# First group of the feed-forward part of a hybrid encoder step: combinations, row sums and row factors in another order

## The reference, cut to what matters

```python
def rmsnorm(x, g, eps=EPS):
    xf = x.astype(jnp.float32)
    y = xf * lax.rsqrt(jnp.mean(xf * xf, axis=-1, keepdims=True) + eps)
    return (y * g.astype(jnp.float32)).astype(x.dtype)

def layer_tail(x, attn, rw, attn_out_g, w_out, norm_ffn_g, w_gate, w_up, w_down):
    mix = jnp.concatenate([rmsnorm(attn, attn_out_g), rw], axis=-1)
    h = x + mix @ w_out
    u = rmsnorm(h, norm_ffn_g)
    return h + (jax.nn.silu(u @ w_gate) * (u @ w_up)) @ w_down
```

## Time and profile before

| | |
|---|---|
| median of 3 runs | 1844.28 us (1843.1 to 1844.76) |
| profiled execution, its own time | 1845.74 us |
| its span, first to last instruction | 1844.0 us |
| mean granted TensorE clock | 0.979 |
| PE busy | 1749.5 us, 95% of the span |
| DVE busy | 959.6 us, 52% |
| POOL busy | 601.8 us, 33% |
| ACT busy | 402.3 us, 22% |

### The profile page before, as it was taken

How to read it: one execution, slowest core, us unless ns; L and a number is a source line. 1 busy time by engine, 2 the same in 40 slices (tenths; PEclk the granted TensorE clock), 3 DMA queues, 4 the chain that set the end, 5 groups by cost and what they waited for, 6 DMA issues and landing times.

```text
span 1844.0 us, 34696 instructions
## 1 busy us (share of the span) xinstructions
PE 1749.5 (95%) x14741; PEld 1327.4 (72%) x14741; DVE 959.6 (52%) x1766; ACT 402.3 (22%) x933; POOL 601.8 (33%) x418
## 2 busy tenths in 40 slices
PE   5999999999997886999999999999999999999998
PEld 4566666666665554666666888888888888888887
DVE  2767767767766774665325344434333334535422
ACT  2333333334333233555001110111001000000000
POOL 3563664555455430001200122211222210734332
PEclk9999999999997888999999999999999999999999
DMA  9443344324322006110402011111011111333431
GB/s 367 142 148 106 88 132 139 97 91 152 99 70 73 8 7 174 47 47 1 186 23 94 23 46 46 46 46 34 35 46 46 46 46 64 123 95 115 141 99 55
DMA packets 80431, 159.00 MB, mean 86 GB/s; under 512 B 28731, under 2 KB 57227, under 8 KB 76054
## 3 DMA queue, kind: packets, MB, share of 16 engines
q1 hardware_dynamic: 76262, 115.81, 19.6%
q10 hardware_dynamic: 4016, 40.96, 6.3%
HBM read 128.60 MB, written 20.48 MB: 81 GB/s over the span
## 4 chain that ended last, share of the span: by engine, by line
PE 50%; DVE 1%; issue 0%; ACT 0%; DVEq 0%
PE psum L2333 45%; PE psum L2312 5%; PE psum L2322 0%; DVE u_sum L2559 0%; DVE mixT L2560 0%; DVE u_sum L2564 0%; PE psum L2328 0%; DVE mixT L2543 0%; DVE rb L2576 0%; DVE hid L2540 0%; DVE hid L2539 0%; DVE hid L2535 0%; DVE yout L2676 0%; DVE part L2675 0%; DVE part L2625 0%
## 5 line engine op out<-in xcount | busy, mean ns | idle before, releaser
L2333 PE MATMUL psum<-mixT,wA 128*128 128x264 f32 x1408 | 338.6, 389 | 1.9 <-DVE rb L2576 1.5
L2333 PEld LDWEIGHTS psum<-mixT,wA 128*128 128x128 f32 x1408 | 269.0, 191 | 48.8 <-DVE rb L2576 1.7
L2333 PE MATMUL psum<-u_sum,wA 128*128 128x264 f32 x1232 | 298.7, 388 | 0.5 <-DVE u_sum L2559 0.5
L461 PE MATMUL psum<-wsl,xt 128*128 128x368 f32 (+1 forms) x1092 | 283.1, 449 | 8.3 <-DMA wsl<-in_w_in 5.0
L2333 PEld LDWEIGHTS psum<-u_sum,wA 128*128 128x128 f32 x1232 | 235.4, 191 | 41.6 <-issue 0.9
L461 PEld LDWEIGHTS psum<-wsl,xt 128*128 128x128 f32 (+1 forms) x1092 | 149.6, 171 | 90.8 <-issue 17.4
L2490 POOL TENSOR_TENSOR wA<-wA 128x512 f32<-128x512 f32 x22 | 27.9, 1268 | 427.9 <-DMA wA<-in_w_gate 231.3
L2333 PE MATMUL psum<-hid,wA 128*128 128x264 f32 x528 | 120.2, 386 | 2.1 <-DVE hid L2627 1.5
L2333 PEld LDWEIGHTS psum<-hid,wA 128*128 128x128 f32 x528 | 100.2, 190 | 19.9 <-issue 2.8
L1956 PE MATMUL psum<-kT,qT 104*128 104x346 f32 (+7 forms) x224 | 77.6, 464 | 10.1 <-DMA kT<-scratch_kT 9.4
L1297 POOL TENSOR_TENSOR Ls<-Lraw,con 128x512 f32<-128x512 f32 x45 | 49.1, 1100 | 95.3 <-ACT Lraw L964 65.2
(11 more groups left out here) (351 smaller groups left out, 2840.7 us busy)
## 6 DMA issues: line engine op xcount, KB each, us to landing
wsl<-in_w_in ACTq DMA_DIRECT2D x27, 1472.0 KB, 6.7
wA<-in_w_down SPq DMA_DIRECT2D x32, 704.0 KB, 4.1
wA<-in_w_gate SPq DMA_DIRECT2D x22, 512.0 KB, 4.3
wA<-in_w_up SPq DMA_DIRECT2D x22, 512.0 KB
mixed<-proj SPq DMA_DIRECT2D x8, 784.0 KB
xt<-in_x_tiles SPq DMA_DIRECT2D x9, 512.0 KB, 6.0
wsl<-in_w_in SPq DMA_DIRECT2D x3, 1472.0 KB, 11.5
out_y<-hid SPq DMA_DIRECT2D x1, 4224.0 KB, 13.9
```

The costliest lines, as they stand in the source:

```text
L461: return pe.matmul(out, lhsT, rhs, start=start, stop=stop)
L2333: ins = pe.matmul(pb[bank][:, 0:NW], left(k), right(k), start=first and k == 0, stop=k == depth - 1, skip_group_check=not first)
```

## The change

Three edits in `tail`, all around the first two groups. (1) DVE does the first group's three combinations before the last block's squares; the squares and the means become `row_means`, called behind the third combination. (2) PE makes the row sums behind the first group's last product, no longer before its closes. (3) The factors are spread by PE transposes of `row_ms` itself, broadcast along a row, against the identity, into banks 5 to 7 and behind X of the second group, not before it; ACT's nine diagonals go. PE signals after four, eight and nine transposes, DVE copies each bank when it is told, and Y, Z and W of the second group wait for the first, second and third copy.

```diff
         def row_factors():
-            pe.wait_ge(s["diag_ok"], TT_)
+            pe.wait_ge(s["r_ok"], 1)
             for t, w in enumerate(width):
-                last = pe.matmul(pb[4 + t // 4][:, t % 4 * P:t % 4 * P + w], ones[0:w, :], diag[0:w, t, 0:w], start=True, stop=True)
-            last.then_inc(s["rb_ps"], 1)
+                last = pe.transpose(pb[5 + t // 4][:, t % 4 * P:t % 4 * P + w], row_ms[0:w, t:t + 1].broadcast_to([w, P]), ident[0:w, 0:w])
+                if t % 4 == 3 or t == TT_ - 1:
+                    last.then_inc(s["rb_ps"], 1)
...
                 if it == 1:
                     pe.wait_ge(s["h_ok"], 3 * KD)
-                    row_factors()
-                    pe.wait_ge(s["rb_ok"], 3)
                 if it >= 2:
                     pe.wait_ge(s["x_done"], it - 1)
                 product(X, left(A11), half(B11u), KH, "p1_ps")
+                if it == 1:
+                    row_factors()
...
+                if it == 1:
+                    pe.wait_ge(s["rb_ok"], 1)
                 if it >= 2:
                     pe.wait_ge(s["y_done"], it - 1)
                 product(Y, left(sw[b][:, 1]), half(T2u), KH, "p6_ps")
...
+                if it == 1:
+                    pe.wait_ge(s["rb_ok"], 2)
                 if it >= 2:
                     pe.wait_ge(s["z_done"], it - 1)
                 product(Z, left(S3), half(B12u), KH, "p7_ps")
                 if it == 0:
-                    row_sums()
                     pe.wait_ge(s["u_hi"], KH)
                 else:
                     pe.wait_ge(s["s1_ok"], u + 1)
+                    if it == 1:
+                        pe.wait_ge(s["rb_ok"], 3)
...
                 product(W, left(sw[b][:, 2]), half(B22u), KH, "w_ps", first=False)
+                if it == 0:
+                    row_sums()
...
                 act.activation(p1_[it % 2][:, :], pb[X][:, 0:NW], ACT.Copy).then_inc(s["p1_ok"], 1)
-                if it == 0:
-                    act.wait_ge(s["r_ok"], 1)
-                    for t in range(TT_):
-                        act.activation(diag[:, t, :], ident, ACT.Copy, scale=row_ms[:, t:t + 1]).then_inc(s["diag_ok"], 1)
...
         tt(T4u, B21u, T2u, ALU.subtract).then_inc(s["t4_ok"], 1)
-        squares(KD - 1)
-        full = TOK // P
-        dve.wait_ge(s["ssq_ps"], 1)
...
+
+        def row_means():
+            squares(KD - 1)
+            full = TOK // P
+            dve.wait_ge(s["ssq_ps"], 1)
...
         def row_factors():
-            dve.wait_ge(s["rb_ps"], 1)
             for n in range(0, TOK, 512):
                 w = min(512, TOK - n)
-                dve.tensor_copy(rb[:, n:n + w], pb[4 + n // 512][:, 0:w]).then_inc(s["rb_ok"], 1)
+                dve.wait_ge(s["rb_ps"], n // 512 + 1)
+                dve.tensor_copy(rb[:, n:n + w], pb[5 + n // 512][:, 0:w]).then_inc(s["rb_ok"], 1)
             dve.wait_ge(s["rb_ok"], 3)
...
                 named(tt(u3, W, u3, ALU.add), "c22_ok", it + 1)
                 if it == 0:
+                    row_means()
                     row_factors()
```

More of the change, by code:

```diff
@@ L2186, in tail @@
     g11 = sb("g11", [P, NW])
-    diag = hid_[:, 9 * TOK:9 * TOK + TT_ * P].rearrange("p (t n) -> p t n", t=TT_)
     ones = hid_[:, 6 * TOK:6 * TOK + P]
@@ L2212, in tail @@
     Alo, Ahi = (w[:, 0:FB * P].rearrange("p (k n) -> p k n", k=FB) for w in wA)
-    names = """x_in0 x_in1 x_in2 g_in in0 in1 in2 in3 lo_read u_hi1 waited zero ps_done h_ok sq_ok acc_ok ssq_ps ms_ok r_ok diag_ok rb_ps rb_ok u_lo u_hi h_st
+    names = """x_in0 x_in1 x_in2 g_in in0 in1 in2 in3 lo_read u_hi1 waited zero ps_done h_ok sq_ok acc_ok ssq_ps ms_ok r_ok rb_ps rb_ok u_lo u_hi h_st
         t1_ok t2_ok t3_ok t4_ok w_in0 w_in1 s1_ok s2_ok s3_ok s4_ok p1_ps p6_ps p7_ps p5_ps x_ps z_ps w_ps
@@ L2564, in _ @@
         tt(T4u, B21u, T2u, ALU.subtract).then_inc(s["t4_ok"], 1)
-        squares(KD - 1)
-        full = TOK // P
-        dve.wait_ge(s["ssq_ps"], 1)
-        dve.tensor_scalar(row_ms[:, 0:full], pb[6][:, 0:full], 1.0 / D, EPS, ALU.mult, ALU.add).then_inc(s["ms_ok"], 1)
-        dve.tensor_scalar(row_ms[0:width[-1], full:], pb[6][0:width[-1], full:TT_], 1.0 / D, EPS, ALU.mult, ALU.add
-                          ).then_inc(s["ms_ok"], 1)
+        def row_means():
+            squares(KD - 1)
+            full = TOK // P
+            dve.wait_ge(s["ssq_ps"], 1)
+            dve.tensor_scalar(row_ms[:, 0:full], pb[6][:, 0:full], 1.0 / D, EPS, ALU.mult, ALU.add).then_inc(s["ms_ok"], 1)
+            dve.tensor_scalar(row_ms[0:width[-1], full:], pb[6][0:width[-1], full:TT_], 1.0 / D, EPS, ALU.mult, ALU.add
+                              ).then_inc(s["ms_ok"], 1)
         def row_factors():
-            dve.wait_ge(s["rb_ps"], 1)
             for n in range(0, TOK, 512):
                 w = min(512, TOK - n)
-                dve.tensor_copy(rb[:, n:n + w], pb[4 + n // 512][:, 0:w]).then_inc(s["rb_ok"], 1)
+                dve.wait_ge(s["rb_ps"], n // 512 + 1)
+                dve.tensor_copy(rb[:, n:n + w], pb[5 + n // 512][:, 0:w]).then_inc(s["rb_ok"], 1)
             dve.wait_ge(s["rb_ok"], 3)
```

## The result

The changed kernel took 1834.33 us in the median of 4 runs (1833.48 to 1837.66), against 1844.52 for the kernel before (1843.1 to 1845.67): a ratio of 0.9948, 95% interval 0.9931 to 0.9966. The profiled execution took 1834.33 us itself, with a span of 1832.5 us and a mean granted clock of 0.981 (0.979 before). The forecast was 1832.8 in a range of 1830.9 to 1836.4.

A forecast was written before the change was run, and what follows sets the result against it. PE bounds the FFN part; the third group's start sets the end. Waits and cheaper factors (4.8 us) plus low clock (6.6) give 11.46 us: profiled execution 1834.3, median 1.46 lower, 1832.8 us; range 1830.9 to 1836.4.

The forecast's parts named there:

- The path: After the third group starts, PE waits for nothing changed; program end moves with that start, from 1038.59 to 1027.13.
- the stretch: PE's time from the start of p7, the first group's last undisturbed product, to the third group's start; 11.46 us less.
- The closes: First group: X, Z, W closes no longer wait for squares; 8.39 us become 5.34, wait of 3.79 becomes 0.39.
- The sums: Row sums behind the first group's last close: no wait, full clock, 1.91 us instead of 3.70.
- The chain to Y: Second group, between X and Y: means, power, transposes, first copy; 0.91 wait, 0.99 transposes, 0.50 wait, replacing 3.83 us.
- The clock: First two groups: 6.6 of the 11.46 us gained are low clock, granted 0.50 after PE's idle times; 1.00 after the change.
- Rival 1: Clock falls again between X and Y of the second group: 1834.6 us for one fall, 1836.4 for two; chance 0.28.
- Rival 2: Cover for ACT's copy of X (0.64 us) or the squares (0.6) too thin: up to 1 us, 1833.8; no own chance.
- Rival 3: PE stays at 1.2 GHz from the sums through the second group and beyond: slower than before, 1851.8 us; chance 0.02.
- Rival 4: First group's closes still held behind the squares; only cheaper factors gain, 1.4 us, 1842.9; chance 0.03.
- The rule weighed: Trainium skill: transposes do not count as busy for the clock; between X and Y they would equal idle time.

The follow-up runs named there:

- the second profile: The kernel before, unedited, profiled again: 32.54 us from p7 of the first group to the third group, 3.20 less than in its first profile.
- the kernel with more sums: The changed kernel with 64 more one-column matmul calls (128 records) ahead of the nine row sums: 1861.92 us.
- the filled kernel before: The kernel before with eight idle matmul calls after p7 and three before the wait for the copies, so PE works through both waits: 1841.28 us, ratio 0.9982.

## Why the prediction was right, and where it was off

**The path.** That only the start of the third group counts held: 805.4 us behind it in both. Forecast 1027.13, measured 1027.03. Part of this closeness is luck: the sum took p7 at 1002.85 from the profile before, and the first profile after had it at the same time, while the next one had it at 1005.12. The length of the stretch, 24.28 forecast and 24.18 measured twice, is not luck.

**The closes.** Close of Z forecast at 1006.80, measured 1006.86; of W 1008.58 and 1008.71. The squares were hidden as said. From the end of u3 on DVE to PE's start it took 0.15 us, not 0.10.

**The sums.** Forecast 1.91 from the attention phase, measured 1.93 (1010.49 to 1012.42).

**The chain to Y.** Power forecast to end at 1014.62, measured 1014.69. I took 0.34 us from there to the first transpose, and it was 0.06: this is the term mis-sized, between its bounds of 0.03 and 0.34. The wait was 0.55 us (1014.20 to 1014.75), not 0.91. The transposes' rate was right, so Y came at 1016.27 for 1016.45.

**The clock.** The 6.6 us of low clock were real in the execution that the prediction read: its sums, closes, X and Y were all at full pace in the changed kernel. Filling the waits gave 4.6 us back against that execution, and the fall left over accounts for most of the rest; against the second profile it gave 1.4. The sum was off in two places. It took the falls of one execution as a fixed part of the kernel before; the second profile had 3.20 us less, so the gain is 8.4 to 11.6 by execution. And the forecast of the time was too low by 1.5 us for another reason: for the profiled execution it was 1834.3, and 1834.33 was measured, but for the median it took off 1.46 more, the distance of one execution before from its median. Nothing tied that distance to the kernel after, whose profiled execution was its own median. One reading was loose: the first fall came at 1007.88, 3.0 us into the wait of 3.56 and not behind it.

**Rival 1** did not occur in any of the seven profiled executions that have all three edits and no added sums, three of them with other work added. Whether it lies behind the longer runs that were not profiled (1837.66, 1839.48) stays open. **Rival 2's** covers held with 0.7 and 0.8 us. **Rival 3** had no trace of itself in the changed kernel. The kernel with more sums shows the half of it that the clock can be low with PE busy, 27.30 us at 1.2 GHz and 1861.92 us in all; the other half, that it does not come back behind products, was seen nowhere. **Rival 4** is excluded by the timeline.

**The rule weighed** (transpose-mode work does not count as busy for the clock, in the Trainium skill, "TensorE: Matmul & The Clock Gate", Part 4) does not hold for these 32-bit transposes: 72 of them in 7.85 us kept the granted clock at 1.00, and in the kernel with more sums it came back while transposes ran.

## What to carry to other kernels

When a matmul engine waits between two bursts, price the wait together with the clock behind it: here 4.8 us of waits and dearer factors came with up to 6.6 us of slow sums and products. A consumer that a reordering exposes must be made fast in the same edit, or the wait only moves. A gain that rests on the clock should be sized from more than one profiled execution of the kernel before; the same stretch had 35.74 us in one and 32.54 in the next.

## What the runs showed of the hardware that was not expected

- One-column matmuls (128x1) do not hold TensorE's clock even back to back: in one kernel it fell 4.66 us into them and stayed at 1.2 GHz while they lasted. At the full clock a record takes 0.107 us, at half 0.205.
- Transposes of a broadcast column cost 0.11 us each at the full clock (72 in 7.85 us, granted clock 1.00) and show as one record each; an ordinary 32-bit matmul call of the same width shows as two.
- The clock fell once behind 2.03 us of sums with PE busy all along (the filled kernel before), and not behind 1.93 us of them in the changed kernel.
- PE started 0.06 us after POOL's power ended (changed kernel). Behind a DVE instruction it started after 0.05 and 0.06 us in the kernel before (squares, last copy) and after 0.15 us twice in the changed kernel (u3, first copy).
